# Order of the tiles in on-chip memory: small tiles first, operands of the large products at multiples of 512 bytes

## What is computed

```python
for l in range(DEPTH):                       # DEPTH = 2
    h = modulate(rmsnorm(x), sh1, sc1)
    z = h @ w_in[l]                          # 1024 x 4512 columns, padded to 36 panels of 128
    ya, yb, yc = spatial_gating(z), latent_attention(z), window_pooling(z)
    merged = g0 * (ya @ w_a[l]) + g1 * (yb @ w_b[l]) + g2 * (yc @ w_c[l])
    x = x + gate1 * (merged @ w_o[l])
    h2 = modulate(rmsnorm(x), sh2, sc2)
    # PEER: 8 heads, each picks 16 of 128 x 128 experts for every token
    x = x + gate2 * sum_k(softmax_k * gelu(u_tab[e_k] . h2)) * v_tab[e_k]
return rmsnorm(x) * final_norm
```

## The kernel before

| tile | start | mod 512 |
|---|---|---|
| `x_sb` | 16,512 | 128 |
| `mov` (and `vrow`, the same place) | 32,896 | 128 |
| `raw` | 65,664 | 128 |
| `whl` | 82,048 | 128 |
| small tiles from `mod` to `rinv` | 114,816 to 123,487 | mixed |
| `identr`, one of them | 119,840 | 32 |
| `sq` (and `hin`, the same place) | 123,488 | 96 |
| `mrg`, `hst` (the same place) | 129,632 | 96 |
| `lat` | 186,976 | 96 |
| `uq` | 197,216 | 96 |
| `htok`, `urow` | 145,952 and 150,048 | 32 |
| `wgt`, `wgthl` | 177,184 and 180,256 | 32 |
| `hot2` (and `gt`, the same place), `hotg` | 209,952 and 218,144 | 32 |

## Time and profile before

### The profile page before, as it was taken

The page is one execution under the profiler, slowest core; times in us unless marked ns, Lnnn a source line. Parts: engine busy times, 40 slices in busy tenths (PEclk is TensorE's granted clock), DMA queues, the critical chain, the costliest instruction groups (busy, mean ns, idle before and its releaser), DMA issues.

```text
span 3511.6 us, 53302 instructions
## 1 busy us (share of the span) xinstructions
PE 3448.3 (98%) x17974; PEld 2925.7 (83%) x17974; DVE 2418.7 (69%) x4725; ACT 1400.6 (40%) x2298; POOL 1372.5 (39%) x1291
## 2 busy tenths in 40 slices
PE   7999999999999999999999999999999999999999
PEld 5776799999999877777777777999999998777777
DVE  6455679999887865555464566899998868555554
ACT  3334244343576332332333333434346753332232
POOL 1011108667743434444400110277668325344442
PEclk9999999999999999999999999999999999999999
DMA  6375447776899989999735743577779999899995
GB/s 239 118 257 183 144 135 228 215 226 189 263 344 324 387 304 350 353 354 348 297 128 178 229 149 130 189 220 207 208 226 278 345 337 368 313 359 350 357 350 185
DMA packets 306403, 910.04 MB, mean 259 GB/s; under 512 B 69076, under 2 KB 101892, under 8 KB 305316
## 3 DMA queue, kind: packets, MB, share of 16 engines
q0 software_dynamic: 163792, 473.58, 39.8%
q1 hardware_dynamic: 105552, 383.83, 31.6%
q10 hardware_dynamic: 36868, 50.35, 3.9%
HBM read 792.14 MB, written 115.47 MB: 258 GB/s over the span
## 4 chain that ended last, share of the span: by engine, by line
PE 90%; DVE 3%; DMA 2%; POOL 2%; issue 2%; ACT 1%; ACTq 0%; SPq 0%; DVEq 0%; POOLq 0%
PE ps L461 15%; PE ps L463 14%; PE ps L462 14%; PE ps L1078 10%; PE ps L1080 10%; PE ps L1079 10%; PE ps L1092 3%; PE ps L1058 3%; PE ps L881 2%; PE ps L978 1%; PE ps L937 1%; PE ps L979 1%; PE ps L980 1%; PE ps L1018 1%; POOL weight_spill L757 1%
## 5 line engine op out<-in xcount | busy, mean ns | idle before, releaser
L461 PE MATMUL ps<-mov,whl 128*128 128x384 f32 (+1 forms) x2816 | 1007.1, 358 | 1.1 <-DVE whl L448 1.1
L463 PE MATMUL ps<-mov,whl 128*128 128x384 f32 (+1 forms) x2816 | 986.7, 350 | 0.0
L462 PE MATMUL ps<-mov,whl 128*128 128x384 f32 (+1 forms) x2816 | 986.1, 350 | 0.0
L448 DVE TENSOR_TENSOR whl<-raw,whl 128x1024 fp32r<-128x1024 f32 x648 | 793.5, 1225 | 220.1 <-ACT whl L438 215.6
L438 ACT CAST whl<-raw 128x1024 fp32r<-128x1024 f32 x648 | 679.7, 1049 | 102.6 <-ACT hst L1273 96.4
L1078 PE MATMUL ps<-whl,wgthl 128*128 128x512 f32 x1536 | 611.3, 398 | 3.4 <-DVE wgthl L1817 3.3
L1080 PE MATMUL ps<-whl,wgthl 128*128 128x512 f32 x1536 | 609.1, 397 | 0.0
L1079 PE MATMUL ps<-whl,wgthl 128*128 128x512 f32 x1536 | 603.8, 393 | 0.0
L461 PEld LDWEIGHTS ps<-mov,whl 128*128 128x128 f32 x2816 | 529.7, 188 | 39.1 <-issue 8.7
L463 PEld LDWEIGHTS ps<-mov,whl 128*128 128x128 f32 x2816 | 529.0, 188 | 31.5
L462 PEld LDWEIGHTS ps<-mov,whl 128*128 128x128 f32 x2816 | 529.9, 188 | 30.2 <-issue 2.2
(11 more groups left out here) (271 smaller groups left out, 3645.5 us busy)
## 6 DMA issues: line engine op xcount, KB each, us to landing
raw<-in_uT_tab SPq DMA_DIRECT2D x256, 512.0 KB, 4.1
raw<-in_v_tab SPq DMA_DIRECT2D x256, 512.0 KB, 6.9
expert_spill<-hst ACTq DMA_DIRECT2D x256, 192.0 KB
hin<-expert_spill POOLq DMA_DIRECT2D x256, 192.0 KB, 7.3
gt<-weight_spill POOLq DMA_DIRECT2D x64, 768.0 KB, 8.6
raw<-in_w_in SPq DMA_DIRECT2D x72, 512.0 KB, 5.4
raw<-in_w_mod SPq DMA_DIRECT2D x64, 512.0 KB, 3.6
weight_spill<-stage POOLq DMA_DIRECT2D x14, 2048.0 KB, 13.3
```

Of the source, the lines that this page charges most:

```text
L448: nc.vector.tensor_tensor(whl[:, m % RING, 1], raw[:, raw_n(m) % RAW], whl[:, m % RING, 0].bitcast(F32), ALU.subtract).then_inc(lo_done, 1)
L461: nc.tensor.matmul(o, w[:, 0, k], src[:, 0, k, :cols], start=(k == 0), stop=False)
L462: nc.tensor.matmul(o, w[:, 0, k], src[:, 1, k, :cols], start=False, stop=False)
L463: mm = nc.tensor.matmul(o, w[:, 1, k], src[:, 0, k, :cols], start=False, stop=(k == KC - 1))
```

## The change

The small tiles are declared ahead of `x_sb`, `mov`, `vrow`, `raw` and `whl`, and the address is then rounded up to a multiple of 512. The tile `mcol`, which nothing used, is gone, and `mx`, `nmx`, `rsum` and `rinv` become four pairs of columns of one tile of 32 bytes. The address is rounded up again ahead of `pick_at`, where `wgt` and `wgthl` begin.

```diff
-    x_sb = sb("x_sb", [P, KC, S])
-    mov_at = top_of[0]
-    mov = sb("mov", [P, 2, KC, S], F32R)
-    vrow = sb("vrow", [P, VR, D], at=mov_at)
-    raw = sb("raw", [P, RAW, KC, P])
-    whl = sb("whl", [P, RING, 2, KC, P], F32R)
     mod = sb("mod_cols", [P, N_MOD])
...
     lnr = sb("lnr", [P, TT])
-    mcol = sb("mcol", [P, 1])
-    mx = sb("mx", [P, 2])
-    nmx = sb("nmx", [P, 2])
-    rsum = sb("rsum", [P, 2])
-    rinv = sb("rinv", [P, 2])
+    rowsm = sb("rowsm", [P, 8])
+    mx, nmx, rsum, rinv = (rowsm[:, 2 * i:2 * i + 2] for i in range(4))
+    top_of[0] += -top_of[0] % 512
+    x_sb = sb("x_sb", [P, KC, S])
+    mov_at = top_of[0]
+    mov = sb("mov", [P, 2, KC, S], F32R)
+    vrow = sb("vrow", [P, VR, D], at=mov_at)
+    raw = sb("raw", [P, RAW, KC, P])
+    whl = sb("whl", [P, RING, 2, KC, P], F32R)
     sq_at = top_of[0]
...
     hin = sb("hin", [P, 4, SD], at=sq_at)
+    top_of[0] += -top_of[0] % 512
     pick_at = top_of[0]
```

## The result

The changed kernel took 3479.12 us, median of 4 runs (3475.12 to 3482.55), against 3513.96 for the kernel before in 4 runs: a ratio of 0.9898, with a 95% interval of 0.9886 to 0.9910. That is 35.8 us faster (31.6 to 40.1); 3484 was forecast, 1.6 us above the slow end of that interval. Its profiled execution took 3476.17 us with a span of 3474.5.

The account below looks back on a forecast made before the run. TensorE's matmul steps were taken as the bound. Terms -30.7 (`weigh`), -2.6 (`mrg`), +1.4 (settling) and +1.0 (`hin`) summed to -30.9 us, from 3514.5 to 3483.6 us; forecast range 3474 to 3516.

Parts of the forecast that it names:

- The bound: Whole kernel: TensorE is busy 3448.3 of 3511.6 us, so the matmuls' steps from start to start decide, not waits.
- weigh: Products of `whl` with `wgthl`: 4608 matmuls were to step at 226.7 instead of 233.3 ns, -30.7 us.
- settling: `weigh` restarting after each pair of quads: slower first steps were to take back +1.4 us.
- mrg: Products of `mrg` with `whl`: 384 matmuls were to step at 226.7 instead of 233.6 ns, -2.6 us.
- mov: Products of `mov` with `whl`: moving these operands from 128 to 0 modulo 512 was taken to change nothing.
- VectorE's 1225 ns: The 1024-column VectorE operation: its 1225 ns was to stay, with zero effect on the time.
- The first panels: First panels of `weigh`: rival that transfers bind there, giving 3489 us; counted into the main case's range, no separate chance.
- The new wait for `hin`: Near 1275: slots of `hin` are used up 0.5 us sooner in each layer, adding +1.0 us.
- the reading of the surplus: `mrg` and `wgthl` products: 6.7 ns extra per matmul, inferred as an operand beginning inside a 64-byte piece.
- Region or roles: Rival for the slow `mrg` and `weigh` steps: region, loop or turned roles, not address; 3514.5 or 3512 us, chance 0.17.
- The larger gain: Rival: up to 10 ns more fall on all 14,000 matmuls, about 3340 to 3410 us; chance 0.09.
- A collision of large operands at the same offset: Rival: TensorE reading `whl` meets ScalarE and VectorE writing its next slot; 9,024 `mov` matmuls pay, 3544 us; chance 0.04.

Follow-up runs that it names:

- wgthl_at_32: The changed kernel with 32 bytes of padding before and after `wgthl`, so that this tile alone begins at 32 modulo 512; ratio 0.9970 to the kernel before.
- all_at_32: The changed kernel with 32 added after both roundings, so all large operands begin at 32 modulo 64; ratio 0.9906 to the kernel before.
- hot_at_32: The changed kernel with the one-hot tiles `hot2` and `hotg` put back to 32 modulo 64; ratio 0.9896 to the kernel before.
- pick_only: The kernel before with only the rounding to 512 ahead of `pick_at`, so `wgt` and `wgthl` go from 32 to 0; ratio 0.9986.

## Why the prediction was right, and where it was not

**The bound and the sizes** held. Steps, not waits, decide. `weigh` was costed at -30.7 + 1.4 for settling: its steps add up to 1046.3 us after and 1073.7 before, -27.4 in the profile over 4,574 of its 4,608 matmuls, and switching `wgthl` alone is worth 29.9 us by the ratios. `mrg` was costed at -2.6: 90.7 to 88.5, -2.2. `mov` at zero: the settled steps are the same. VectorE's 1225 ns stayed (1224). The first panels now carry 379 GB/s, 377 were forecast, and do not bind. The new wait for `hin` was put at +1.0 us; the waits for `wgthl` rose from 3.3 to 5.4, but they run from 2.3 to 7.8 in the other profiles with no relation to their speed, so that term can't be confirmed by itself.

**The step that failed is the reading of the surplus**: "It is what one more piece of 64 bytes would cost if the operand were read in such pieces and began inside one." With both operands 32 bytes past a multiple of 64 the step is 226.7; with neither, at a distance of 128, it is 233.3. The rows of before had three kinds of pairs, and I described each by the start of its odd tile. They are described as well by the distances 0, 32 and 160, and nothing in them decides between the two. The number came out by luck in this respect: the change sets every start to 0 modulo 512, which also sets every distance to 0. Had it aligned `wgthl` alone, this reasoning would have promised 30 us and 5 had come.

**The rivals.** Region or roles fell with `wgthl_at_32`. The larger gain did not come: none of the distances tried gives less than 226.7 ns, and 0, 32, 64 and 128 as starts with distance 0 give the same. So the 13.3 ns over 512 / 2.4 GHz follow no start and no distance that was tried; what they are stays open. A collision of large operands at the same offset did not come either: the same offset is the good case.

On the pages: the Trainium skill, "SBUF — State Buffer", section "Specifications (TRN2)", with its 16-byte lines, would have nothing change. For starts alone the steps agree with it (226.7 ns with all operands at 32, at 64 and at 0; the ratios are 0.9906, 0.9903 and 0.9885 to 0.9898); it does not speak of two operands against each other, and there `wgthl_at_32` measured 6.7 ns per matmul.

**What is left of the gain.** Of the profile's 37.1 us, `weigh` and `mrg` explain 29.6. From the first one-hot matmul to the first of `weigh`, the two layers took 228.9 + 226.7 = 455.6 us before and 222.8 + 224.4 = 447.2 after. In the twelve other profiles this stage took 447.4 to 453.7, with no relation to the distances of the product there, so part of it is that the one profile of before has the longest value. A part may be a transfer: the median time from issue to landing of the 2 MB of `stage` is 13.3 us before and 12.5 after. It is 15.0 in `all_at_32`, where `stage` begins at 32 as it does in the kernel before, so the start alone does not set it. The rows of the DMA issues (count, KB each, us to landing) of before, of after and of `all_at_32`:

```profile
weight_spill<-stage POOLq DMA_DIRECT2D x14, 2048.0 KB, 13.3
```

```profile
weight_spill<-stage POOLq DMA_DIRECT2D x14, 2048.0 KB, 12.5
```

```profile
weight_spill<-stage POOLq DMA_DIRECT2D x14, 2048.0 KB, 15.0
```

In the first layer one such transfer stands on the path near 975 in both profiles (13.43 us before, 12.60 after); in the second layer one does after (11.52) and none before. Over the fourteen profiles the stage took 447.2 to 451.6 us with `stage` at a multiple of 256 and 450.0 to 455.6 without, means 2.5 us apart with values that overlap. The ratios lean the same way. With all distances at 0, the three kernels with `stage` off a multiple of 256 stand at 0.9903, 0.9906 and 0.9914, the changed kernel and `hot_at_32` at 0.9885 to 0.9898, some 5 us apart in the mean.

`pick_only`, 5 us faster than before, says little on this, since its `weigh` steps at about 232.7 ns and not 233.3, some 3 us in sum. `wgthl_at_32`, with `stage` at 0, says more: its `weigh` steps as before and it is 10.5 us faster by the ratio, of which `mrg` explains 2.2. Its expectation had put 2.6 to 5 us there. The transfer is argued, not shown, and some 5 to 8 us of the result stay without a settled cause.

## What to carry to other kernels

When two operands of float32r matmuls with 512 moving columns are placed, make their starts equal modulo 256. It made no difference to the step to what: 0, 32, 64 and 128 were tried, always with pieces that begin multiples of 512 bytes after their tile. Two paddings of less than 256 bytes each were worth 0.9% here. To find such a price, take the step from start to start, not the duration, and compare kinds that differ in one thing; and before naming the cause, write down every property in which they differ, since here start and distance had changed together.

## What the runs showed of the hardware

- The step of a float32r matmul with its own 128 x 128 stationary load is N / 2.4 GHz + 13.3 ns at distance 0 modulo 256 (226.7 at 512 columns, 173.3 at 384), with both starts at 0, 32, 64 or 128.
- At 512 columns other distances cost 6.0 to 6.7 ns (32, 64, 128, 160, 224) or 2.2 ns (192). At 384 columns 32 costs nothing, 64 costs 3.3 and 128 costs 2.5 ns. Multiples of 32 are what was tried. What in the chip makes it so stays open.
- At distance 0 the step settles within some ten matmuls after other work: in the profile after, `weigh` steps at 234.5 ns in the mean just after a pause or other work and at 226.7 from the tenth step on. At other distances it does not come down to that: in the profile before, `weigh` is still at 233.3 beyond the twenty-fourth step.
- The 2 MB from `stage` landed in 12.5 to 12.7 us (median of the 14 of a profile) when it began at a multiple of 256 and in 13.3 to 15.4 us when it did not, in the profiles of all kernels. The Trainium skill, "DMA: Bandwidth & Descriptors", section "How a descriptor splits into AXI transactions", says that the first transaction of a descriptor that does not start at a multiple of 256 bytes begins at the boundary below, and that the bytes fetched ahead of the start still cost beats, its unit of transfer. The rows agree in direction; no run here shows the transactions.
